# Chunkwise opening of a two-block transformer kernel, with the decays moved to block 1

## What is computed

```python
h = rmsnorm(x, g_pre[i])
proj = h @ w_in[i]          # 2048 x 18464
qkv, z_a, b_raw, a_raw, ... = jnp.split(proj, ...)
qkv = silu(causal_depthwise_conv(qkv, w_conv_qkv[i]))   # 4 taps
q, k, v = l2norm(heads(q)), l2norm(heads(k)), heads(v)  # 16 heads of 128
beta = sigmoid(b_raw)
g_log = -exp(a_log) * softplus(a_raw + dt_bias)         # the decays
o_a = gated_delta_chunked(q, k, v, g_log, beta)
```

## Time and profile before

| | us |
|---|---|
| median of 3 runs (2110.65 to 2110.95) | 2110.89 |
| the profiled execution | 2111.19 |
| its span in the profile | 2109.4 |
| TensorE busy | 2086.9 |
| VectorE busy | 1480.2 |
| ScalarE busy | 1234.4 |
| GpSimd busy | 337.7 |

### The profile page before, as it was taken

One profiled execution on the slowest core, in us unless ns is written; L12 is line 12 of the kernel. 1 busy time (PEld: TensorE's weight loads), 2 busy tenths in 40 slices (PEclk: granted clock), 3 DMA queues, 4 the chain that ended last, 5 costly groups with the idle time before them and its releaser, 6 DMA issues.

```text
span 2109.4 us, 28764 instructions
## 1 busy us (share of the span) xinstructions
PE 2086.9 (99%) x9881; PEld 1742.1 (83%) x9881; DVE 1480.2 (70%) x2691; ACT 1234.4 (59%) x2368; POOL 337.7 (16%) x468
## 2 busy tenths in 40 slices
PE   7999999999999999999999999999999999999998
PEld 6888888888888888888888888888888888888886
DVE  6777777789999987579665665655665745456666
ACT  6666666677777764457555555544554555555543
POOL 1111111156666641010000000000000000000000
PEclk9999999999999999999999999999999999999999
DMA  8877776779877866576777664655656555644462
GB/s 249 233 216 208 203 206 191 216 214 274 225 215 210 234 210 218 193 269 211 260 263 250 223 217 171 214 180 182 237 209 205 184 187 187 196 160 140 140 239 100
DMA packets 434690, 439.69 MB, mean 208 GB/s; under 512 B 27728, under 2 KB 306384, under 8 KB 432144
## 3 DMA queue, kind: packets, MB, share of 16 engines
q1 hardware_dynamic: 412752, 381.76, 58.5%
q0 software_dynamic: 7600, 35.79, 4.9%
q10 hardware_dynamic: 14224, 20.71, 2.7%
HBM read 410.92 MB, written 27.28 MB: 208 GB/s over the span
## 4 chain that ended last, share of the span: by engine, by line
PE 98%; DVE 1%; DMA 0%; ACT 0%; SPq 0%; issue 0%; DVEq 0%
PE pair L480 29%; PE pair L482 29%; PE pair L481 29%; PE QA L1511 1%; PE RA L1527 1%; PE RA L545 1%; DMA raw<-in_w_in_dram 0%; PE QB L1596 0%; PE RB L1502 0%; PE pair L502 0%; PE pair L501 0%; PE pair L500 0%; PE RB L815 0%; PE RA L820 0%; PE RA L807 0%; PE QA L534 0%
## 5 line engine op out<-in xcount | busy, mean ns | idle before, releaser
L461 DVE TENSOR_TENSOR w_lo<-raw,w_hi 128x512 fp32r<-128x512 f32 x1368 | 915.5, 690 | 365.4 <-ACT w_hi L454 363.2
L454 ACT ACTIVATE w_hi<-raw 128x512 fp32r<-128x512 f32 x1368 | 825.4, 625 | 427.1 <-PE pair L482 421.5
L480 PE MATMUL pair<-w_hi,in_hi 128*128 128x512 f32 x2336 | 929.9, 398 | 1.6 <-DVE w_lo L461 1.6
L482 PE MATMUL pair<-w_hi,in_lo 128*128 128x512 f32 x2336 | 911.2, 390 | 0.0
L481 PE MATMUL pair<-w_lo,in_hi 128*128 128x512 f32 x2336 | 909.7, 389 | 0.0
L482 PEld LDWEIGHTS pair<-w_hi,in_lo 128*128 128x128 f32 x2336 | 438.4, 188 | 93.5
L480 PEld LDWEIGHTS pair<-w_hi,in_hi 128*128 128x128 f32 x2336 | 438.9, 188 | 88.4 <-DVE w_lo L461 2.4
L481 PEld LDWEIGHTS pair<-w_lo,in_hi 128*128 128x128 f32 x2336 | 439.2, 188 | 86.8
L1047 POOL TENSOR_TENSOR acc_p<-acc_p,tap 128x256 f32<-128x256 f32 x160 | 183.9, 1150 | 37.3 <-ACT tap L1021 23.9
L1021 ACT ACTIVATE tap<-upad,cwl 128x256 f32<-128x256 f32 x192 | 96.6, 508 | 51.6 <-POOL acc_p L1047 50.3
L1078 DVE SCALAR_TENSOR_TENSOR QB<-upad,cwl,QB 128x256 f32<-128x256 f32 x272 | 120.2, 485 | 0.0
(11 more groups left out here) (428 smaller groups left out, 1854.4 us busy)
## 6 DMA issues: line engine op xcount, KB each, us to landing
raw<-in_w_in_dram SPq DMA_DIRECT2D x512, 256.0 KB, 3.9
raw<-in_w_in_dram SPq DMA_DIRECT2D x80, 1024.0 KB, 5.2
raw<-in_w_out_dram SPq DMA_DIRECT2D x48, 1024.0 KB, 5.0
raw<-in_w_kv_shared_dram SPq DMA_DIRECT2D x24, 1024.0 KB, 5.0
raw<-in_w_br_a_dram SPq DMA_DIRECT2D x16, 1024.0 KB, 6.4
raw<-in_w_br_b_dram SPq DMA_DIRECT2D x16, 1024.0 KB, 7.2
raw<-in_w_mem_kv_dram SPq DMA_DIRECT2D x16, 1024.0 KB, 5.0
raw<-in_w_ple_gate_dram SPq DMA_DIRECT2D x16, 1024.0 KB, 5.0
```

The lines of the kernel that those rows point to most:

```text
L454: act.activation(piece(blk, q)[0], raw[:, u, q % UK], ACT.Copy).then_inc(hi_ready[u], 1)
L461: dve.tensor_tensor(lo, raw[:, u, q % UK], hi.bitcast(F32), ALU.subtract).then_inc(lo_ready[u], 1)
L480: pe.matmul(o, xh, wh, start=(q == 0), stop=False)
L482: mm = pe.matmul(o, xl, wh, start=False, stop=(q == KC - 1))
```

## The change

The first weights are loaded chunk by chunk (`load_first`), one transfer of 256 KB for all four column slices, at most four on their way, as each waits for ScalarE's split of the chunk four before it. x comes in two pieces of two chunks and three of four, the first three from ScalarE's queue, the other two from SP's between weight chunks. ScalarE and VectorE split x in pairs between the first weight chunks, and TensorE starts with block 0 itself and waits for each pair of x chunks before its use. The ba split, the squares and their sums come later in block 0; the ba products stand behind half-chunks 18 and 24, their transposition behind 30, the squares behind 31. Mean, power and decays move to block 1: `means_dve` at VectorE's half 0, `decays_dve` at 2 and its last part at 15, `decays_act` at ScalarE's 3 and its last part at 13, `decays_pe` behind TensorE's half-chunk 11, the wait for `head_ready` behind 25. Its PSUM banks are now RA and RB. Head 0's keys are five half-chunks later on all three engines. The transfers of `gc_rows` and `gc_b` go from SP to GpSimd's `keys_pool` of head 0, and block 1's loads also wait for the high halves of block 0's last unit. GpSimd's loads of the channel columns start after the fourth x pair, not the eighth.

```diff
-    def load_heads(sp, blk, base, h, behind={}):
+    def load_heads(sp, blk, base, h):
...
+            if isinstance(blk, int) and blk == 1:
+                sp.wait_ge(hi_ready[UNITS - 1], u + 1)
...
-            for transfers in behind.get(u, ()):
-                transfers(sp)
...
+    def load_first(sp):
...
+        for q in range(KC):
+            if q >= UNITS:
+                sp.wait_ge(hi_ready[(q - UNITS) // UK], (q - UNITS) % UK + 1)
+            sp.dma_start(raw[:, q // UK, q % UK].rearrange("p (g n) -> p g n", g=4),
+                         w_in[:, q, COL_A:COL_A + 4 * D].rearrange("p (g d) -> p g d", g=4)[:, :, 0:P]).then_inc(w_loaded[q % UNITS], 16)
+            if q in (3, 5):
+                c = q // 2 - 1
+                sp.wait_ge(s["cols_hi"], c + 1)
+                x_quarter(sp, 2 + c, c)
...
     def hi_piece(act, blk, q):
...
-        if q % UK == 0:
+        if isinstance(blk, int) and blk == 0:
+            act.wait_ge(w_loaded[q % UNITS], 16 * (q // UNITS + 1))
+        elif q % UK == 0:
...
     def keys_pool(pool, h, par):
-        reach(pool, s["decay_diff"], h - 1)
...
-        pool.tensor_copy(hst[:, par], head_all[:, bass.ds(h, 1)].rearrange("p a n -> p (a n)"))\
-            .then_inc(s["head_staged"], 1)
...
+        if isinstance(h, int) and h == 0:
+            decays_pool(pool)
+        reach(pool, s["decay_diff"], h - 1)
+        pool.tensor_copy(hst[:, par], head_all[:, bass.ds(h, 1)].rearrange("p a n -> p (a n)"))\
+            .then_inc(s["head_staged"], 1)
+        if isinstance(h, int) and h == 0:
+            decays_back_pool(pool)
+            b_buffers_pool(pool)
...
+    X_IN = [("x_in0", 32), ("x_in1", 16)] + 2 * [("x_in2", 16)] + 2 * [("x_in0", 48)] + 2 * [("x_in1", 32)]
...
     def split_x_act(act, groups):
...
-            act.wait_ge(s[f"x_in{g // 4}"], 16)
+            act.wait_ge(s[X_IN[g][0]], X_IN[g][1])
...
     def start_sp(sp):
-        sp.dma_start(chan[:, CH_GPRE:CH_GPRE + KC], t["g_pre"]).then_inc(s["gain_in"], 16)
...
-    def second_half_sp(sp):
-        sp.dma_start(x_cols[:, KC // 2:KC], t["x_columns"][:, KC // 2:KC]).then_inc(s["x_in1"], 16)
+        sp.dma_start(chan[:, CH_GPRE:CH_GPRE + KC], t["g_pre"]).then_inc(s["x_in0"], 16)
...
+    def x_quarter(eng, c, i):
+        k = slice(4 * c, 4 * c + 4)
+        eng.dma_start(x_cols[:, k], t["x_columns"][:, k]).then_inc(s[f"x_in{i}"], 16)
...
     def columns_loads_pool(pool):
...
-        pool.wait_ge(s["cols_hi"], KC // 2)
+        pool.wait_ge(s["cols_hi"], KC // 4)
...
-    def decays_sp(sp):
-        sp.wait_ge(s["gc_copied"], 3)
-        sp.dma_start(gc_rows, gcT[:, :]).then_inc(s["gc_stored"], 16)
-        sp.wait_ge(s["gc_stored"], 16)
-        sp.wait_ge(s["head_ready"], 1)
-        sp.wait_ge(s["ba_done"], 2)
-        sp.dma_start(gc_b[:, :, :], gc_rows.partition_broadcast(P)).then_inc(s["gc_stored"], 16)
...
-    def start_pe(pe):
-        for g in range(KC // 4):
-            decays_first_pe(pe, g)
...
-    def start_last_pe(pe):
-        for g in range(KC // 4, KC // 2):
+    def decays_pool(pool):
+        pool.wait_ge(s["gc_copied"], 3)
+        pool.dma_start(gc_rows, gcT[:, :]).then_inc(s["gc_stored"], 16)
+        pool.wait_ge(s["head_ready"], 1)
...
+    def decays_back_pool(pool):
+        pool.wait_ge(s["gc_stored"], 16)
+        pool.wait_ge(s["ba_done"], 2)
+        pool.dma_start(gc_b[:, :, :], gc_rows.partition_broadcast(P)).then_inc(s["gc_stored"], 16)
...
+    def decays_halves_pe(pe, c):
+        for g in range(c * KC // 4, (c + 1) * KC // 4):
...
     def decays_pe(pe):
...
-        pe.matmul(QA[:, 0:2 * HEADS], triu, sgl[:, 15], start=True, stop=True)
-        pe.matmul(QB[:, 0:2 * HEADS], ones, sgl[:, 15], start=True, stop=True).then_inc(s["gc_done"], 1)
+        pe.matmul(RA[:, 0:2 * HEADS], triu, sgl[:, 15], start=True, stop=True)
+        pe.matmul(RB[:, P:P + 2 * HEADS], ones, sgl[:, 15], start=True, stop=True).then_inc(s["gc_done"], 1)
...
-        pe.transpose(QA[0:TT * HEADS, 0:P], sgl[:, 0], ident).then_inc(s["gcT_done"], 1)
+        pe.transpose(RA[0:TT * HEADS, P:2 * P], sgl[:, 0], ident).then_inc(s["gcT_done"], 1)
     def start_act(act):
+        for g in range(2):
+            k = slice(2 * g, 2 * g + 2)
+            act.dma_start(x_cols[:, k], t["x_columns"][:, k]).then_inc(s[f"x_in{g}"], 16)
+        x_quarter(act, 1, 2)
...
-        act.dma_start(x_cols[:, 0:KC // 2], t["x_columns"][:, 0:KC // 2]).then_inc(s["x_in0"], 16)
...
-        act.wait_ge(s["gain_in"], 16)
...
+    def ba_split_act(act):
...
-        split_x_act(act, range(KC // 4))
...
+    def decays_last_act(act):
...
-        dve.tensor_copy(v(0), QA[:, 0:2 * HEADS]).then_inc(s["gc_copied"], 1)
+        dve.tensor_copy(v(0), RA[:, 0:2 * HEADS]).then_inc(s["gc_copied"], 1)
...
-        dve.tensor_tensor(v(1), QB[:, 0:2 * HEADS], v(0), ALU.subtract).then_inc(s["gc_copied"], 1)
+        dve.tensor_tensor(v(1), RB[:, P:P + 2 * HEADS], v(0), ALU.subtract).then_inc(s["gc_copied"], 1)
...
-        dve.tensor_copy(gcT[:, :], QA[0:TT * HEADS, 0:P]).then_inc(s["gc_copied"], 1)
+        dve.tensor_copy(gcT[:, :], RA[0:TT * HEADS, P:2 * P]).then_inc(s["gc_copied"], 1)
...
+    def decays_last_dve(dve):
+        hv = head_all[:, :, :].rearrange("p h (k t) -> p k t h", t=TT)
...
     def _(sp):
...
-        load_heads(sp, 0, COL_A, 0, {0: (second_half_sp,)})
+        load_first(sp)
...
-        decays_sp(sp)
...
-    MEANS_DVE, SQUARES_PE, DECAYS_DVE, DECAYS_ACT, DECAYS_PE = 13, 17, 16, 19, 25
+    X_ACT = {4: 3, 5: 7, 6: 11, 7: 15}
+    SQUARES_ACT = (9, 13, 17, 19)
+    SUMS_DVE = (18, 22, 24, 26, 28)
+    FIRST_KEYS = 5
+    later = lambda f: lambda h, par, hs: f(h, par, hs - FIRST_KEYS)
...
     def _(pe):
...
-        start_pe(pe)
-        pe_block(pe, 0, 0, in_hi, in_lo, begins(pe, {8: start_last_pe, 13: decays_turn_pe, SQUARES_PE: squares_pe, DECAYS_PE: decays_pe}))
-        pe.wait_ge(s["head_ready"], 1)
-        pe_block(pe, 1, 1, in_hi, in_lo, beside([(keys, 0, 0)]))
+        pe.wait_ge(s["cols_lo"], 1)
+        next_pair = {4 * g - 1: lambda pe, g=g: pe.wait_ge(s["cols_lo"], g + 1) for g in range(1, KC // 2)}
+        pe_block(pe, 0, 0, in_hi, in_lo, begins(pe, {**next_pair, 18: lambda pe: decays_halves_pe(pe, 0), 24: lambda pe: decays_halves_pe(pe, 1),
+                                                     30: decays_turn_pe, 31: squares_pe}))
+        decays = lambda _, par, hs: begins(pe, {11: decays_pe, 25: lambda pe: pe.wait_ge(s["head_ready"], 1)})(hs)
+        pe_block(pe, 1, 1, in_hi, in_lo, beside([(later(keys), 0, 0), (decays, 0, 0)]))
...
-            if q == UK:
-                square_act(act, 0)
-                square_act(act, 1)
-                split_x_act(act, range(KC // 4, KC // 2))
+            if q % 2 == 0:
+                split_x_act(act, (q // 2,))
...
-        act_block(act, 0, begins(act, {0: lambda act: square_act(act, 2), 2: lambda act: square_act(act, 3), DECAYS_ACT: decays_act}))
-        act.wait_ge(s["x_rms"], 2)
-        act_block(act, 1, beside([(keys, 0, 0)]))
+        split_x_act(act, (AHEAD // 2,))
+        x_pairs = {hs: lambda act, g=g: split_x_act(act, (g,)) for g, hs in X_ACT.items()}
+        squares = {hs: lambda act, n=n: square_act(act, n) for n, hs in enumerate(SQUARES_ACT)}
+        act_block(act, 0, begins(act, {**x_pairs, **squares, 5: ba_split_act}))
+        decays = lambda _, par, hs: begins(act, {3: decays_act, 4: lambda act: act.wait_ge(s["x_rms"], 2), 13: decays_last_act})(hs)
+        act_block(act, 1, beside([(decays, 0, 0), (later(keys), 0, 0)]))
...
-        start_dve(dve)
...
-            if q == UK:
-                square_sum_dve(dve, 0)
-                split_x_dve(dve, range(KC // 4, KC // 2))
+            if q % 2 == 0:
+                split_x_dve(dve, (q // 2,))
...
-        dve_block(dve, 0, begins(dve, {2: products_dve, **{2 * n + 2: lambda dve, n=n: square_sum_dve(dve, n) for n in range(1, 5)}, MEANS_DVE: means_dve, DECAYS_DVE: decays_dve}))
+        split_x_dve(dve, (AHEAD // 2,))
+        x_pairs = {hs + 1: lambda dve, g=g: split_x_dve(dve, (g,)) for g, hs in X_ACT.items()}
+        sums = {hs: lambda dve, n=n: square_sum_dve(dve, n) for n, hs in enumerate(SUMS_DVE)}
+        dve_block(dve, 0, begins(dve, {**x_pairs, **sums, 6: decays_first_dve, 30: products_dve}))
...
-        dve_block(dve, 1, beside([(keys, 0, 0)]))
+        decays = lambda _, par, hs: begins(dve, {0: means_dve, 2: decays_dve, 15: decays_last_dve})(hs)
+        dve_block(dve, 1, beside([(decays, 0, 0), (later(keys), 0, 0)]))
...
-        pool.wait_ge(s["head_ready"], 1)
...
-        b_buffers_pool(pool)
```

More of the change, by code:

```diff
@@ L373, in program @@
     psum_ready, psum_free = sem("psum_ready"), sem("psum_free")
-    names = ("chan_in", "gain_in", "x_in0", "x_in1", "cols_hi", "cols_lo", "x_summed", "ba_in", "consts_in", "x_ss", "x_rms",
+    names = ("chan_in", "x_in0", "x_in1", "x_in2", "cols_hi", "cols_lo", "x_summed", "ba_in", "consts_in", "x_ss", "x_rms",
```

(4 more changed lines are left out.)

## The result

The changed kernel takes 2115.64 us in the median (2113.13 to 2117.16) against 2111.06 (2110.46 to 2111.53) for the kernel before, measured beside it: a ratio of 1.0020, interval 1.0012 to 1.0028. It is 4.6 us slower, where 1 us gained was forecast, and lies outside the range. Its profiled execution took 2116.09 us with a span of 2114.3, 4.9 more than the span before. A few executions, of the kernel before (2627.66 us) as of others, ran at a lower granted clock from end to end, and are in no range given here.

A forecast was written before the change was run, and what follows sets the result against it. TensorE was taken as the bound, busy 2086.9 us, 99% of the span. Terms 2.2 + 1.6 - 0.3 - 2.7 = 0.8, some 1 us off the median 2110.89, gave 2109.9; range 2105.3 to 2114.5.

The forecast's parts named there:

- The new start: Opening: weight chunk 0 lands at 6.8, TensorE starts at 8.2 instead of 10.41; gain 2.2 us (-0.5 to +4.1).
- my own signs: Wrong if L540's silu wait is missing, first load lands outside 6 to 7.5, or TensorE waits after block 2 starts.
- Supply of block 0: Block 0's weight loads, four in flight, just keep pace: 0.5 us idle against 2.1 removed; gain 1.6 us (-1.9 to +2.1).
- Rival (b): Opening starves: late start at 10.9, TensorE loses 3 to 4 us between chunks 2 and 9; 2117.7 us, chance 0.10.
- The clock ... nothing in the sum: Opening: the half-speed stretch moves to block 0's own matmuls, 1.5 us lost instead of 1.4, so no net change.
- The decays in block 1: Block 1: TensorE loses 0.3 us to ScalarE's copies and 2.7 (0 to 4) waiting for head 0's silu.
- Z: Start of the squares, 31.87 us before the change, now at the end of block 0; block 1's times count from it.
- the move to GpSimd: The two gc transfers leave SP's queue; gc_b lands near Z + 27, wanted at Z + 30 or later; nothing charged.
- Rival (c): Clock falls to 1.2 GHz in block 1's 2.7 us wait, its rise costing about 1.4 us again; 2111.3, chance 0.07.
- the moved ba work: Block 0: ba's split, squares and sums cost nothing, as ScalarE and VectorE run up to eight chunks ahead of TensorE.

The follow-up runs named there:

- mix2: mix1 with ScalarE's third x piece and ba_raw also issued later, behind its first weight split; 2108.01 us, ratio 0.9986 to the kernel before.
- mix1: Changed kernel with head 0's keys eight half-chunks late, decays_pe behind half-chunk 9, GpSimd's broadcasts later, VectorE's ba copy at half 25; 2110.05 us, ratio 0.9995.

## Why the prediction was wrong, step by step

**The new start: right in direction, under-rated.** 7.45 against 8.2, inside the bounds. The weights of chunk 0 landed near 5.9 and were split from 5.95 on, where I had them land at 6.8. Gain 3.0 instead of 2.2. By my own signs the forecast was in doubt here: a first load outside 6 to 7.5 was one, if barely, and a wait behind the start of block 2 another (0.4 at L1010).

**"Supply of block 0": wrong, and at another place than I looked.** I charged 0.5 us for a ring of four that just keeps pace. The ring did keep pace: behind chunk 1 TensorE never waited for weights again. What I had not priced is the second transfer. I shared out the DMA engines for chunk 0, and then took chunks 1 to 3 as following in step. They stood against the rest of x, ba_raw and the broadcasts, and chunk 1 came 5.3 us later than chunk 0: 2.5 us lost instead of 0.5. Rival (b) had the sign and 3 to 4 us of stops, but with a late start and a starved ring, and neither happened.

**"The clock ... nothing in the sum": wrong.** I took the low stretch as a fixed 1.5 us that only changes its place. A stop inside it can prolong it: with 2.28 us of idling 14 more matmuls ran at half speed, 4.0 us lost in all, 2.5 more than I had. With 1.37 (the broadcasts later) none did. The length of the stop alone doesn't decide it: 14 ran slow behind 1.74 and 1.80 us, some 8 to 9 behind 1.66 and 1.89. Even without a stop 2.0 were lost (mix2: about ten matmuls at 0.2 each), as the low stretch lasted 4.0 us (7.31 to 11.3) and not the 3.0 of before (10.41 to 13.38); why, stays open.

**The decays in block 1: right in every mechanism.** ScalarE's copies 0.2 for 0.3; VectorE free at Z + 10.95 for 11.2 (52.90 less 41.95); nothing at half 11 but 0.3 at L1266, which the trace of before has at L1246 too; the silu done at Z + 23.35 for 23.7; the wait 2.47 for 2.7. No wait of TensorE shows a cost of the move to GpSimd, as charged.

**Rival (c) was true, and I gave it 0.07.** The fall behind the silu wait cost 1.7 for my 1.4, and it showed in every profile with a wait of 2.5 us for that silu, and in none where it was 1.6 or less. I kept it apart because the 1.6 us of the earlier trace rows had not brought it about, which was true of that length alone. The rule of the Trainium skill (TensorE: Matmul & The Clock Gate, Part 1), that the clock falls after idle time, agrees with these traces: full behind 1.6 us of idling, 0.50 behind 2.47.

**A bound that no step had: the ba copy behind block 1's first weights.** I counted the moved ba work as hidden inside block 0, by the engines' lead. The lead is what hurts: an engine six chunks ahead has the next block's weights before the last items of this one in its list, and SP's gate makes these late. In the changed kernel the copy, at 40.0 us, just met TensorE, so it cost nothing there; but where the opening was repaired with the copy still at half 30, TensorE waited 2.65 and 3.2 us for it, which is why single repairs seemed worthless.

By terms, in spans: start +0.8 better than forecast, chunk 1 -2.0, opening clock -2.6, silu and copies +0.1, clock behind the silu -1.7, L1010 -0.4, together -5.8, to the 5.7 between the 0.8 that the sum gained and the 4.9 lost. The 0.3 of the opening and the 0.3 of block 1 that I can't place cancel.

## What to carry to other kernels

Price a stop of TensorE twice, once as idle time and once as the matmuls at half speed behind it, also while it still runs at the low level. When the first of several equal transfers is made early, work out the second and the third as well, with all that is in flight beside them. An item placed late in the list of an engine that runs ahead stands behind the next block's loads; when a repair gains nothing, look for such an item before giving the repair up.

## What was unexpected in the hardware

- The views show the granted clock as 1.00 in the opening while the steps are double (8.01 to 9.72 in the timeline above), but 0.50 for the same steps at 66 to 70 us. The view does show 0.50 for them at 12 to 16 us in the kernel with the warm-up, where TensorE had reached full speed before. Until it first has, only the steps tell.
- The changed kernel spreads over 4.0 us, and the one with x and the broadcasts later over 6.5 (2110.52 to 2117.06), while mix1, mix2 and, but for one execution at 2113.06, the kernel before stay within 1 to 2. My reading is that the clock's fall and rise vary from one execution to the next; the opening shows it (14 or 8 slow matmuls behind like stops), the rest is not shown.
- Two transfers of equal size that SP issued one behind the other were ready at 5.95 and 11.22 us. With 0.75 MB of ScalarE's queue issued later, they were ready within 1.5 us of each other, and with the broadcasts later too, both by 7.1. The Trainium skill (DMA: Bandwidth & Descriptors, Issuing engines are not separate DMA queues) says that transfers of all issuing engines interleave on the same 16 DMA engines. These runs agree: block 0's sixteen transfers of 256 KB took 2.9 to 10.3 us to land in the changed kernel.
- Left open: why the kernel with the keys eight half-chunks late scatters over 4.5 us though its profiled execution shows no fall, and the 0.3 us in the opening that no row explains. The mean granted clock of its two longest executions (2117.24 and 2118.01) is 0.997 and of the nine others 0.998, which would fit a fall in those two, but they have no trace.
